# Attention over 16 heads ahead of a mixture of experts: order of VectorE's and TensorE's steps, and places of the first expert weights

## What is computed

```python
s = (einsum(q_nope, k_nope) + einsum(q_rope, k_rope)) * scale
s = where(causal, s, -inf)
p = softmax(s, axis=-1)
outs.append(einsum('bhqk,bkhd->bqhd', p, v[:, :qe]))
o = concatenate(outs, axis=1).reshape(B, S, N_HEADS * V_HEAD_DIM)
f = o @ w_o
x = layer_norm(DEEPNORM_ALPHA * x + f, ln_g[i, 0], ln_b[i, 0])
f = hier_moe(x, ...)                      # router, then silu(x w1) * (x w3) @ w2 per expert
# second model, for each of its layers:
kv = einsum('bmd,dn->bmn', rmsnorm(mem, g_mem), w_mem_kv)   # keys | values
```

## Time and profile before

| | us |
|---|---|
| median of 3 runs | 2265.2 (2264.96 to 2267.9) |
| the profiled execution, its own time | 2263.17 |
| its span, first to last instruction | 2261.4 |
| PE busy | 1922.7 (85%) |
| PEld busy | 1270.4 (56%) |
| DVE busy | 485.1 (21%) |
| ACT busy | 367.0 (16%) |
| DMA, mean over the span | 262 GB/s |
| mean granted TensorE clock | 0.94 of 2.4 GHz |

### The profile page before, as it was taken

The page is one execution under the profiler, slowest core; times in us unless marked ns, Lnnn a source line. Parts: engine busy times, 40 slices in busy tenths (PEclk is TensorE's granted clock), DMA queues, the critical chain, the costliest instruction groups (busy, mean ns, idle before and its releaser), DMA issues.

```text
span 2261.4 us, 34483 instructions
## 1 busy us (share of the span) xinstructions
PE 1922.7 (85%) x15190; PEld 1270.4 (56%) x15190; DVE 485.1 (21%) x1024; ACT 367.0 (16%) x847; POOL 23.7 (1%) x27
## 2 busy tenths in 40 slices
PE   8698777777767876777666999999999999999998
PEld 5456554555545654555543868555544868646553
DVE  5331111111135111111113022322022013312022
ACT  4321100111102100111111112221111012222111
POOL 1000000000000000000000000000000000000000
PEclk9899998889888988988888999999999999999999
DMA  8468999999995999999994433532443433343340
GB/s 331 94 245 344 419 421 420 420 420 420 420 393 235 411 420 421 420 421 420 420 405 159 157 137 113 187 129 90 180 159 120 175 136 135 123 158 112 121 149 19
DMA packets 142153, 592.23 MB, mean 262 GB/s; under 512 B 14128, under 2 KB 15536, under 8 KB 92208
## 3 DMA queue, kind: packets, MB, share of 16 engines
q1 hardware_dynamic: 135520, 567.43, 63.5%
q0 software_dynamic: 6480, 22.55, 3.4%
HBM read 580.51 MB, written 9.44 MB: 261 GB/s over the span
## 4 chain that ended last, share of the span: by engine, by line
PE 54%; DMA 24%; SPq 10%; DVE 8%; ACT 2%; issue 1%; DVEq 0%; ACTq 0%
DMA ring<-in_moe_w_dram 23%; PE ps L464 22%; PE ps L453 10%; SPq L847 4%; PE ps L1053 4%; SPq L852 3%; SPq L848 3%; PE ps L410 3%; PE ps L459 2%; PE ps L436 2%; PE ps L382 2%; ACT arena L556 1%; PE ps L1035 1%; PE ps L1086 1%; PE ps L1300 1%
## 5 line engine op out<-in xcount | busy, mean ns | idle before, releaser
L1053 PE MATMUL ps<-ring,xT 128*32 128x128 f32 x8192 | 310.3, 312 | 196.5 <-DMA ring<-in_moe_w_dram 195.0
L464 PE MATMUL ps<-ring,xT 128*128 128x512 f32 x960 | 421.5, 595 | 0.7 <-ACT xT L533 0.7
L1053 PEld LDWEIGHTS ps<-ring,xT 128*32 128x32 f32 x8192 | 268.3, 124 | 262.1 <-DMA ring<-in_moe_w_dram 211.3
L453 PE MATMUL ps<-xT,ring 128*128 128x256 f32 x1408 | 309.8, 380 | 0.0
L464 PEld LDWEIGHTS ps<-ring,xT 128*128 128x128 f32 x960 | 180.9, 191 | 211.6 <-issue 209.8
L453 PEld LDWEIGHTS ps<-xT,ring 128*128 128x128 f32 x1408 | 266.1, 190 | 39.2 <-issue 4.9
L1086 PE MATMUL ps<-arena 128*32 128x512 f32 x768 | 118.7, 606 | 31.3 <-DVE arena L1681 31.3
L1035 PE MATMUL ps<-arena,x_tm 128*128 128x128 f32 x1024 | 138.3, 292 | 5.2 <-DVE arena L1666 4.5
L1681 DVE TENSOR_TENSOR arena<-arena,ps 128x256 f32<-128x256 f32 x32 | 13.5, 421 | 583.6 <-ACT arena L1387 583.6
L1035 PEld LDWEIGHTS ps<-arena,x_tm 128*128 128x128 f32 x1024 | 129.7, 206 | 15.3 <-issue 10.6
L1379 ACT COPY arena<-ps 128x512 f32<-128x512 f32 x32 | 18.7, 585 | 640.4 <-PE ps L1053 640.4
(11 more groups left out here) (250 smaller groups left out, 1440.3 us busy)
## 6 DMA issues: line engine op xcount, KB each, us to landing
ring<-in_moe_w_dram SPq DMA_DIRECT2D x288, 1024.0 KB, 26.2
ring<-in_w_in_dram SPq DMA_DIRECT2D x52, 2048.0 KB, 8.2
arena<-in_moe_w_dram SPq DMA_DIRECT2D x96, 1024.0 KB, 27.0
ring<-in_w_mem_kv_dram SPq DMA_DIRECT2D x4, 2048.0 KB, 19.1
ring<-in_w_br_diff_dram SPq DMA_DIRECT2D x4, 2048.0 KB, 7.9
ring<-in_w_out_dram SPq DMA_DIRECT2D x4, 2048.0 KB, 8.5
ring<-gap_bias POOLq DMA_DIRECT2D x4, 1536.0 KB, 9.9
gap_bias<-gap_rows POOLq DMA_DIRECT2D x1, 5120.0 KB, 46.8
```

Of the source, the lines that this page charges most:

```text
L453: m = nc.tensor.matmul(bank[:, u * T:(u + 1) * T], w[:, k, f * P:(f + 1) * P], xT[:, k, :], start=(k == 0), stop=(k == KD - 1))
L464: m = nc.tensor.matmul(bank, x_[:, k, half * P:(half + 1) * P], w[:, k, :], start=(k == 0), stop=(k == KD - 1))
L1053: m = nc.tensor.matmul(ps[SL * q:SL * q + SL, g % 2, s * P:(s + 1) * P], xs[:, g % 2, k, s * SL:(s + 1) * SL], w[:, c0:c0 + 2 * P - 1:2], ...
```

## The change

Four edits, made together.

1. On DVE `norm_p(h)` comes ahead of `mask(h + 2)`.
2. On PE all 32 memory-key matmuls stand between the heads, two per step: one ahead of `turn(h)` and one after `values(h - 1)`. The call after the first logits is gone.
3. The tenants of `ring` change places: `w_o` in slots 0 and 1, the key weights in slot 2, the value weights in slot 3, the memory itself in slot 4. Layer 1's places are the same as before.
4. SP's list follows: down 0 and 1, then (after `mkv_ps` 2) up 2, then down 2 to 7; up 0 and 1 after `w_o`; up 3 after the memory values; up 4 after `mk_out`.

```diff
-        wo, qT = places(ring, 3 * UPW, RINGW, (KD, D), (NH, T))
+        wo, qT = carve(ring, 0, KD, D), carve(ring, UPS * UPW, NH, T)
...
-        mem_tm, memT = places(ring, 2 * UPW, 3 * UPW, (TT, D), (KD, T))
+        mem_tm, memT = places(ring, 4 * UPW, 5 * UPW, (TT, D), (KD, T))
...
-        memT_of = [carve(ring, 2 * UPW, KD, T), carve(ring, 3 * UPW, KD, T)]
-        mk_w = [carve(ring, 0, KD, CW), carve(ring, UPW, KD, CW)]
-        mv_w = [carve(ring, UPW, KD, CW), carve(ring, 2 * UPW, KD, CW)]
-        mk_new = [carve(ring, s * UPW + KD * T, MH, T) for s in (2, 3)]
+        memT_of = [carve(ring, 4 * UPW, KD, T), carve(ring, 3 * UPW, KD, T)]
+        mk_w = [carve(ring, 2 * UPW, KD, CW), carve(ring, UPW, KD, CW)]
+        mv_w = [carve(ring, 3 * UPW, KD, CW), carve(ring, 2 * UPW, KD, CW)]
+        mk_new = [carve(ring, s * UPW + KD * T, MH, T) for s in (4, 3)]
...
             sp.wait_ge(sem("o_ps"), NH)
-            for e in range(DNS):
+            load_down(sp, 0, 0)
+            load_down(sp, 0, 1)
+            sp.wait_ge(sem("mkv_ps"), 2)
+            load_up(sp, 0, 2)
+            for e in range(2, DNS):
                 load_down(sp, 0, e)
             sp.wait_ge(sem("f_ps"), 4)
-            load_up(sp, 0, 3)
-            load_up(sp, 0, 4)
-            sp.wait_ge(sem("mkv_ps"), 2)
             load_up(sp, 0, 0)
+            load_up(sp, 0, 1)
             sp.wait_ge(sem("ln_done"), 1)
             load_ln(sp, 0, 1, gain, shift)
             sp.wait_ge(sem("mkv_ps"), 4)
-            load_up(sp, 0, 1)
+            load_up(sp, 0, 3)
             sp.wait_ge(sem("mk_out"), 16)
-            load_up(sp, 0, 2)
+            load_up(sp, 0, 4)
...
                 if h < NH:
                     if h == 0:
                         pe.wait_ge(sem("qT_ready0"), 4)
-                    mem_keys(pe, 0, 0, 6, h, h + 1)
+                    if h == 8:
+                        pe.wait_ge(sem("qT_ready1"), 4)
+                    half = h // 8
+                    mem_keys(pe, 0, half, 6 + half, 2 * (h % 8), 2 * (h % 8) + 1)
                     turn(h)
                 if h >= 1:
                     values(h - 1)
-                if 8 <= h < NH:
-                    if h == 8:
-                        pe.wait_ge(sem("qT_ready1"), 4)
-                    mem_keys(pe, 0, 1, 7, h - 8, h - 7)
+                if h < NH:
+                    mem_keys(pe, 0, half, 6 + half, 2 * (h % 8) + 1, 2 * (h % 8) + 2)
...
             pe_logits(pe, 0, 0)
-            mem_keys(pe, 0, 1, 7, KD)
             pe.wait_ge(sem("ln_part"), 2)
...
             for h in range(NH):
+                norm_p(h)
                 if h + 2 < NH:
                     mask(h + 2)
-                norm_p(h)
```

## The result

| | before | after |
|---|---|---|
| median | 2265.08 us (4 runs, 2264.59 to 2267.9) | 2243.85 us (4 runs, 2241.66 to 2245.08) |
| the profiled execution, its own time | 2263.17 | 2245.08 |
| its span | 2261.4 | 2243.3 |

The ratio is 0.9902 with a 95% interval of 0.9887 to 0.9917: the medians are 21.2 us apart. (The ratio isn't the quotient of the two medians, which is 0.9906 and lies inside the interval.) 2242.8 was forecast, with a range of 2238 to 2253.

What follows compares the result with a forecast made beforehand. Expert-weight DMA bounds layer 0, its start set by PE's list up to `mkv_ps` 4. 25.0 - 2.6 + 0 = 22.4 us off 2263.2 gives 2240.8; the median, 2.0 above, 2242.8, range 2238 to 2253.

Steps and rivals of the forecast that it cites:

- Bound now: Layer 0's experts are bound by DMA bytes, so only an earlier stream start, dated by `mkv_ps` 4, moves their end.
- Part 1: Heads, new DVE order: PE becomes the bound at 2.83 us a step; end 101.0 against 126.0, a gain of 25.0 us.
- the long low stretch: Heads of the kernel before, 60.4 to 77.3: clock at 0.50; if it came back in full, 8.5 us of gain gone.
- I take full clock: Heads: PE has work through most of the low-clock stretch after the change, so its steps were priced at full clock.
- its allowance: Heads: 0.6 us added to the computed end of 100.4 for waits that don't mesh.
- Part 2: Router: moving eight memory keys away leaves PE idle about 5.0 us and the clock falls, a loss of 2.6 us.
- The row of layer 1: Layer 1's same steps without keys, after 5.99 us of idle PE: 7.12 us against 4.55 in layer 0.
- Part 3: New `ring` places and SP's list: stream restarts at the same distance plus 2.6 us; taken as 0, bounds 0 to 2.6 gained.
- The hole: Layer 0's expert stream in the kernel before, 193.5 to 198.5: DMA share 0.47, 2.6 us lost.
- Everything shifts: Behind the heads and router, both layers' streams and the second model move by the whole gain, 22.4 us.
- Low clock in part of the heads: Rival, chance 0.14: low clock returns in part of the heads, price up to 8.5 us, 2244 to 2251.
- the others: Rivals: another loop sets the step (0.10), clock holds or hole closes (0.10), DVE edit idle (0.04), heads at half clock (0.03).

Runs made afterwards that it cites:

- e1: The changed kernel with the order on DVE undone, mask(h + 2) ahead of norm_p(h) again: 2267.68 us, ratio 1.0009 to the kernel before.
- e2: The kernel before with only the two DVE calls exchanged, nothing else: 2236.16 us, ratio 0.9874 to the kernel before.
- e7: The kernel before with the new DVE order and all memory keys between the heads, old places kept: 2243.81 us, ratio 0.9896.
- e3: The changed kernel with memory keys placed as before (24 between heads, 8 behind the first logits), SP's list accordingly: 2237.71 us, ratio 0.9882.
- e9: The changed kernel with layer 1's route weights issued ahead of the wait for the memory values: 2236.93 us, ratio 0.9871 to before.
- e10: The kernel before with the new DVE order and layer 1's route weights ahead of the wait for the memory values: 2232.59 us, ratio 0.9851.
- e4: The changed kernel with four matmuls of unread result added in PE's idle time behind the first logits: 2241.20 us, ratio 0.9897.
- e11: The changed kernel itself, run again unaltered in the last session, on another chip than the earlier runs: 2241.32 us, ratio 0.9886.
- e6: The changed kernel with five memory-value products moved into PE's idle time behind the first logits: 2237.07 us, ratio 0.9867.
- e8: The kernel before with the new DVE order, 11 keys behind the first logits, layer 1's route weights at expert 16: 2235.89 us, ratio 0.9863.

## Why the prediction was right

**Bound now.** Right. The stage is bound by the bytes of the experts. Moving the date of `mkv_ps` 4 moved the end: 21.5 us at that date, 19.4 deep in the stage.

**Part 1, 25.0 us.** Right, with the cause shown by e1 and e2. The step is 2.84 us, forecast 2.83. The end was forecast at 101.0 and came at 101.8. The sum was 0.8 short because of a low clock in the first step and a half. That the long low stretch would go was in the sum as "I take full clock", but its worth, some 5 of the 25 us, was not set apart. In the repeat run without that low clock the first down weights went out at 100.26, where the sum without its allowance had 100.4.

**Part 2, 2.6 us lost.** Right in cause, and in size for the profiled execution (7.21 - 4.55 = 2.66). Over six traces it is 1.5 to 2.8 us. The row of layer 1 was the right stand-in. What the step didn't draw is its consequence. The eight keys cost PE about 3.5 us between the heads *and* their old place had been free. By the medians this edit costs 7.7 us with the old places (e7 against e2) and, with the new ones, 6.1 or 3.6 (the change or its repeat, against e3). In one session, with the places, it is 4.3 us (e9 against e10). The sum had both terms, but I never set the change against the version without this edit.

**Part 3, 0 with up to 2.6 gained.** The value for the places was right within 2 us (e3 against e2, e7 against the change). The bound was on the wrong side. The hole did not close or stay, it grew from 2.6 to about 4.3 us in the profiled execution, and the range for this term had nothing below zero. In the sum it is an error of 1.7 us. The growth goes with the new places: measured alike, the hole is 3.4 us in e1, e3, e4 and e11 and 3.1 in e6, but 2.6 to 2.9 in e2 and e7, which have the old ones. Part of it is visible: in the changed kernel the last route issue is held 1.27 us and not 0.43, and the experts' issues come 0.9 us later. The rest isn't explained.

**What lies behind.** "Everything shifts" was not exact. 1.2 us went in the second model's first products (13.19 us for 24 matmul records, 11.96 before), which run behind 18.9 us of idle PE (18.2 before) at a low clock. In ten of the eleven other traces, with e1 among them, they take 12.9 to 13.5 us, in e4 12.1. So the kernel before has the odd value, and whether the change has a part in that isn't shown. The closeness of the total is in part luck. The profiled execution was forecast at 2240.8 and took 2245.08, 4.3 us more, which is these misses together. The median was put 2.0 us above the profiled execution, as in the kernel before, but it came 1.2 below. Those 3.2 us in the other direction leave 1.05.

**The rivals.** Low clock in part of the heads came true for about 3 of 17 us, at a price of 1.5 and not 8.5. None of the others did. The remark of part 2 that the trace bears out the loss only for long waits holds for 77.5 to 96, but the fall in the heads before came behind waits of 2.10 us and less and lasted 17 us.

## What to carry to other kernels

In a loop over stages on in-order engines, put the instruction that the next engine is waiting for ahead of the one that prepares two steps later: the swap of two calls was worth 29 us of 2265. Once a stage is full, any filler in it is paid for. Filler belongs where the engine waits for something else, and here it was worth more there than its own length (4.3 us moved, 5.8 to 6.9 gained in the list), because it also kept the clock up. Set a change of several edits against the version with the strongest edit alone. And look at what stands behind a full DMA queue in the issuer's list: here some 300 KB in pieces of 32 and 256 B held it until the queue had run dry.

## What was not expected of the hardware

- **Small transfers behind a full queue held the issuing engine long enough to empty the DMA engines.** With 4 MB queued the group bias took 11.86 us to issue, and 4.3 us of stream were lost. In the full stream two of the four route issues took 18.57 and 4.38 us, with 3.7 lost. With an empty queue the group bias took 0.66 us and nothing was lost, and behind the last up weights (e10) it took 2.71. The hold alone doesn't make a hole: in the middle of the changed kernel's stream SP is held 6.29 us in the issue of a 1 MB down weight, at a DMA share of 1.02 from 370 to 377. Which of the four route transfers, and whether their size or their number of pieces, makes the difference isn't separated. While these transfers pass, the rate is low though the engines are busy: 204 GB/s at a share of 1.09 from 171 to 173. The Trainium skill ("DMA: Bandwidth & Descriptors", section "Specifications") gives 512 B as the least transfer size for full rate; the rows of the route weights are 32 and 256 B, and the trace agrees on the low rate.

```profile
171.00:173.00 2.00, 2.00 (x36) 1.79 (x28) 0.00 (x0) 0.58 (x1) 0.00 (x0) 1.00 1.09 204
```

```profile
370.55 6.29 SPq L852 DMA_DIRECT2D arena<-in_moe_w_dram  x1
```

- **The low clock in the heads isn't a fixed cost.** Before, it was 17 us at 0.50 with PE busy 13.4 of 16.9. In e1_mask_first, with the same chain of waits and one key more in it per step, it was 3 to 4 us. With the new order on DVE six traces had about 3 us, and five (e2, e3, e8, e9, e11) none. Two kernels with the same heads, e2 and e10, ended them at 97.66 with none and at 99.32 with 3 us. For the order before there is one trace, so whether its 17 us are usual isn't known. A stage that begins with waits can lose several microseconds or none, and a forecast should carry it as a range.
